# State-space outputs from four partial products, combined in PSUM by TensorE

## What is computed

```
_, _, x_re, x_im = lax.associative_scan(_ssm_combine, (a_re, a_im, bu_re, bu_im), axis=0)
y = (jnp.einsum('bsgp,ghp->bsgh', x_re, c_re.astype(f32))
     - jnp.einsum('bsgp,ghp->bsgh', x_im, c_im.astype(f32)))
y = y.reshape(bsz, s, S5_WIDTH) + d_skip.astype(f32) * uf
```

## Time and profile before

| | |
|---|---|
| time, median of 3 runs | 2228.7 us (2225.8 to 2232.6) |
| profiled execution, its own time | 2228.75 us |
| its span, first to last instruction | 2226.9 us |
| mean granted TensorE clock | 0.986 of full speed |
| busy: TensorE, VectorE, ScalarE, GpSimd | 97%, 68%, 45%, 32% |
| the four heads with state-space work | about 133 to 375 us of the span |

### The profile page before, as it was taken

One profiled execution on the slowest core, in us unless ns is written; L12 is line 12 of the kernel. 1 busy time (PEld: TensorE's weight loads), 2 busy tenths in 40 slices (PEclk: granted clock), 3 DMA queues, 4 the chain that ended last, 5 costly groups with the idle time before them and its releaser, 6 DMA issues.

```text
span 2226.9 us, 47155 instructions
## 1 busy us (share of the span) xinstructions
PE 2165.3 (97%) x18426; PEld 2134.6 (96%) x18426; DVE 1508.2 (68%) x1798; ACT 1005.2 (45%) x1244; POOL 708.4 (32%) x668
## 2 busy tenths in 40 slices
PE   8898889999999999999999999999999999999997
PEld 8888789999999999999999989999999999999997
DVE  6688896677666555666666666677666555666665
ACT  5333334545444444444444455444544444444442
POOL 4687771023434101434311000124343002343311
PEclk9999999999999999999999999999999999999998
DMA  6334334455555556545456433455554556454453
GB/s 261 141 138 145 125 137 172 160 198 176 207 192 191 169 195 215 201 177 206 162 195 219 161 120 136 161 201 190 185 198 177 182 198 215 184 207 180 173 192 116
DMA packets 64602, 398.68 MB, mean 179 GB/s; under 512 B 7168, under 2 KB 9728, under 8 KB 29056
## 3 DMA queue, kind: packets, MB, share of 16 engines
q1 hardware_dynamic: 60192, 391.15, 49.2%
q10 hardware_dynamic: 4320, 6.27, 0.9%
HBM read 395.29 MB, written 2.10 MB: 178 GB/s over the span
## 4 chain that ended last, share of the span: by engine, by line
PE 92%; DVE 4%; DVEq 2%; ACT 1%; issue 0%; DMA 0%; SPq 0%; ACTq 0%
PE PS L1492 27%; PE PS L1493 27%; PE PS L1496 27%; DVE lo L722 1%; DVEq L932 1%; PE PS L1590 1%; PE PS L1639 1%; PE PS L1487 1%; PE PS L1488 1%; PE PS L1489 1%; PE PS L1641 1%; PE PS L1640 1%; DVE S L948 1%; PE PS L1604 1%; ACT hi L363 0%
## 5 line engine op out<-in xcount | busy, mean ns | idle before, releaser
L722 DVE TENSOR_TENSOR lo<-raw,hi 128x1024 fp32r<-128x1024 f32 (+2 forms) x826 | 966.9, 1189 | 516.4 <-ACT hi L363 511.1
L363 ACT ACTIVATE hi<-raw 128x1024 fp32r<-128x1024 f32 (+2 forms) x826 | 787.2, 970 | 798.5 <-PE PS L1496 722.8
L1492 PE MATMUL PS<-XS,hi 128*128 128x256 f32 x3584 | 843.8, 278 | 8.6 <-ACT hi L363 8.6
L1493 PE MATMUL PS<-XS,hi 128*128 128x256 f32 x3584 | 838.4, 277 | 0.0
L1492 PEld LDWEIGHTS PS<-XS,hi 128*128 128x128 f32 x3584 | 674.3, 188 | 12.0 <-issue 11.6
L1493 PEld LDWEIGHTS PS<-XS,hi 128*128 128x128 f32 x3584 | 674.4, 188 | 0.4
L1496 PE MATMUL PS<-XS,lo 128*128 128x256 f32 x3584 | 481.0, 277 | 0.0
L1496 PEld LDWEIGHTS PS<-XS,lo 128*128 128x128 f32 x3584 | 441.4, 188 | 0.0
L1493 PE MATMUL PS<-YF,hi 128*128 128x256 f32 x1408 | 331.8, 276 | 0.0
L1492 PE MATMUL PS<-YF,hi 128*128 128x256 f32 x1408 | 331.8, 276 | 0.0
L1449 POOL TENSOR_TENSOR ctmp<-apad,cws 128x512 f32<-128x512 f32 x88 | 131.9, 1519 | 525.7 <-DVE apad L773 525.7
(11 more groups left out here) (259 smaller groups left out, 2465.0 us busy)
## 6 DMA issues: line engine op xcount, KB each, us to landing
raw<-in_ffn_up SPq DMA_DIRECT2D x176, 1024.0 KB, 4.8
raw<-in_ffn_dn SPq DMA_DIRECT2D x128, 704.0 KB, 4.1
raw<-in_w_in SPq DMA_DIRECT2D x51, 1024.0 KB, 4.8
raw<-in_w_oe SPq DMA_DIRECT2D x16, 1024.0 KB, 4.8
raw<-in_w_oo SPq DMA_DIRECT2D x16, 1024.0 KB, 4.8
raw<-in_mla_dn SPq DMA_DIRECT2D x9, 1024.0 KB, 4.8
raw<-in_w_ukv SPq DMA_DIRECT2D x8, 1024.0 KB, 4.7
raw<-in_w_uq SPq DMA_DIRECT2D x8, 768.0 KB, 4.3
```

The source lines that it names most:

```text
L363: act.activation(hi[:, p % SLOTS, 0:n], raw[:, u % SLOTS, off:off + n], ACT.Copy).then_inc(hi_ready, 1)
L722: V.tensor_tensor(lo[:, p % SLOTS, 0:n], raw[:, u % SLOTS, off:off + n], f(hi[:, p % SLOTS, 0:n]), ALU.subtract).then_inc(lo_ready, 1)
L1492: mm(PS[:, bank, 0:T], wh, x[:, 0:T], start=first, stop=False)
L1493: mm(PS[:, bank, 0:T], wh, x[:, T:2 * T], start=False, stop=False)
```

## The change

`Cst` gets a third plane. GpSimd writes the negated real part into it and the negated imaginary part over plane 1, as before; the load now writes runs of 64 values into a wider row. VectorE no longer forms the difference and the sum (L955, L956) nor the drain ahead of them, and raises `z_ready` behind the second product. `c_x` takes the four products as they are: C_re times s_re cos, -C_re times s_im sin, -C_im times s_re sin, -C_im times s_im cos, four matmuls per block instead of two, and goes through the two blocks in turn. Since `sB` is now read by `c_x`, the copy of new inputs into `sB` (bu_copy for an even m) waits for `c_done` of the half before and not for `z_ready`.

```
-        Cst = sb("Cst", [P, 4, 2, 32], fp32, even)
+        Cst = sb("Cst", [P, 4, 3, 32], fp32, even)
...
-                    act.dma_start(Cst[:, :, :, :].rearrange("p a b c -> p (a b c)"),
-                                  A["s5c"][h0 - 1, :, :] if r is None else
-                                  A["s5c"][ds(r + (h0 - 1), 1), :, :].rearrange("a p n -> p (a n)")).then_inc(cst_in, 16)
+                    act.dma_start(Cst[:, :, 0:2, :],
+                                  (A["s5c"][h0 - 1, :, :] if r is None else
+                                   A["s5c"][ds(r + (h0 - 1), 1), :, :].rearrange("a p n -> p (a n)"))
+                                  .rearrange("p (a b c) -> p a b c", a=4, b=2)).then_inc(cst_in, 16)
 
                 def bu_copy(m):
                     act.wait_ge(bu_done, S_(m + 1, 4))
                     if m % 2 == 0 and h0 - 1 + m > 0:
-                        act.wait_ge(z_ready, S_(m // 2, 2))
+                        act.wait_ge(c_done, S_(m // 2, 2))
...
                     V.tensor_tensor(sT2, sT1, eb[:, 0:1].broadcast_to([P, 2, 2, T]), ALU.mult)
-                    V.tensor_tensor(sB, sT1, eb[:, 1:2].broadcast_to([P, 2, 2, T]), ALU.mult)
-                    dve.drain()
-                    V.tensor_tensor(sT1[:, 0], sT2[:, 0], sB[:, 1], ALU.subtract)
-                    V.tensor_tensor(sT1[:, 1], sT2[:, 1], sB[:, 0], ALU.add).then_inc(z_ready, 1)
+                    V.tensor_tensor(sB, sT1, eb[:, 1:2].broadcast_to([P, 2, 2, T]), ALU.mult).then_inc(z_ready, 1)
...
                 pool.wait_ge(cst_in, at(16 * h0 + 16, 16, r))
+                G.tensor_tensor(Cst[:, :, 2, :], Cst[:, :, 0, :], minus[:, 0:1].unsqueeze(2).broadcast_to([P, 4, 32]),
+                                ALU.mult)
                 G.tensor_tensor(Cst[:, :, 1, :], Cst[:, :, 1, :], minus[:, 0:1].unsqueeze(2).broadcast_to([P, 4, 32]),
                                 ALU.mult).then_inc(cneg_ready, 1)
...
-                    for m in range(2):
-                        q = 2 * k + m
-                        for ri in range(2):
-                            ins = mm(PS[32 * q:32 * q + 32, 6, 0:T], Cst[:, q, ri, :], sT1[:, ri, m, :],
-                                     start=ri == 0, stop=ri == 1)
+                    for i, (c, x) in enumerate(((0, sT2[:, 0]), (2, sB[:, 1]), (1, sB[:, 0]), (1, sT2[:, 1]))):
+                        for m in range(2):
+                            q = 2 * k + m
+                            ins = mm(PS[32 * q:32 * q + 32, 6, 0:T], Cst[:, q, c, :], x[:, m, :], start=i == 0, stop=i == 3)
```

## The result

The changed kernel takes 2207.0 us (median, 2202.3 to 2210.1) against 2230.7 us (2225.8 to 2236.3) for the kernel before in the same comparison: a ratio of 0.9889, interval 0.9876 to 0.9902, or some 24 us less. I had forecast 11 us less; the time lies at the lower edge of my range of 2207 to 2229. The sign was right and the size was half of what came, because one step of the sum carried a duration over unchanged that didn't stay, and the count of half-clock spells hung on that step.

A forecast was written before the change was run, and what follows sets the result against it. VectorE's run up to c_x(0), and half clock behind TensorE's waits, were taken as the bound. Head 1 -1.7 - 3.3, matmuls +4.4, three turns -7.2, one spell -3.3: -11.1 us, 2217.5 us; range 2207 to 2229.

The forecast's parts named there:

- What bounds the kernel: TensorE waits 18.4 us in four places, c_x(0) of heads 1 to 4, for VectorE's sum, and restarts at half clock.
- Sums removed: Ahead of c_x(0): without L955, L956 and the drain, z_ready comes 1.73 us earlier in head 3.
- Matmuls added: In c_x on TensorE: doubled matmuls take 1.86 us, 0.87 more, at five exposed places: +4.4 us.
- Rival (c): In c_x: the new order stops matmuls running two at a time, 2.5 us more each; 2237 us, chance 0.07.
- (d): In c_x: the new order runs more matmuls at a time, so c_x stays at 0.99 us; 2213 us, chance 0.08.
- Wait added: At b_u(1) in heads 2 to 4: moving bu_copy(0) behind c_x(1) makes TensorE stand 0.75 us, out of slack.
- VectorE's run: VectorE's work up to c_x(0) ends last in a turn; heads 2 to 4 gain 2.4 us each by it.
- the walk: VectorE's run followed in head 3's times: L1029 0.7 us instead of 2.78, scan(0) 0.8 us early, z_ready at 259.5.
- The step that failed: From scan(0) to the end of L953 on VectorE: 7.66 us, as before.
- outer bound: Gain per turn if scan to L953 shrank from 7.66 to head 1's 5.99 us: about 4.1 us.
- The half clock: Behind c_x(0): head 1 keeps full clock, 3.3 us; one of three later spells goes, another 3.3 us.
- Rival (b): Heads 1 to 4: all half-clock spells go; 2211 us, up to 2207 with 3 us or more a turn; chance 0.20.

The follow-up runs named there:

- e1_sums_away: Kernel before without the two sums and their drain, end rotation left out of the result; 0.9905 of the kernel before, 21 us less.
- e8_sums_kept: Changed kernel with the drain, difference and sum kept ahead of z_ready, their result unused; 0.9958 of the kernel before, 9 us less.
- e6_block_by_block: Changed kernel with the eight matmuls of c_x issued block by block instead of in turn; 0.9912 of the kernel before.
- e12_sums_and_wait: Kernel before with sums away and bu_copy's wait moved, c_x keeping four matmuls, end rotation left out; 0.9894 of the kernel before.
- e3_wait_only: Kernel before with only the wait of bu_copy moved from z_ready to c_done; 0.9947 of the kernel before, 12 us less.
- e7_phasors_later: Changed kernel with GpSimd waiting for z_ready of the first half before making the second half's phasors; 0.9928 of the kernel before.
- e9_gpsimd_later: Kernel before with five tiny GpSimd writes ahead of the products of rotate_in(0) in heads 2 to 4; 0.9935, 14 us less.
- e4_clock_kept: Kernel before with six or eight unused full-width matmuls filling the idle time ahead of c_x(0); 0.9947, 12 us less.
- e2_matmuls_only: Kernel before with every matmul of c_x issued twice, sums and waits as before; 0.9953 of the kernel before, 10 us less.

## Why the prediction was half of it

**What bounds the kernel**: right. The time sat in four waits for VectorE and in the clock behind them.

**Sums removed**, 1.73 us a turn: right. In the changed kernel z_ready comes with the end of the product and TensorE follows 0.13 us later. I hadn't seen that this part decides: alone it gives 21 us (e1_sums_away), and the other two without it give 9 (e8_sums_kept).

**Matmuls added**, 1.86 us per c_x: right, 1.85 to 1.92. That they run two at a time in the new order was right; e6_block_by_block shows that the order isn't indifferent. Rival (c) didn't come, nor did (d), whose 0.99 us no c_x of sixteen records reached. What they cost in time, my +4.4 us, no run shows: e12_sums_and_wait has half of them and the same time.

**Wait added**, 0.75 us at b_u(1): right, 0.70. That it goes into slack was right, and said too little: alone it makes the kernel 12 us faster (e3_wait_only), since it starts GpSimd later.

**VectorE's run**, up to the scan: the direction was right, and L1027 at 0.69 us as walked. The scan came 1.26 us earlier against c_x(1), I had 0.8. Three readings were off: L1029 was ready at 237.3 and not at 236.3 (it starts at 237.34 in the earlier trace rows), GpSimd's first product came 1.9 us later against c_x(1) and not 1.65, and the walk's own 0.8 and 1.73 make 2.53 us a turn where the sum took 2.4.

**The step that failed** is the next one: "Then 7.66 us to the end of L953, as before". It was 5.78 to 6.0 us in all three heads. I had that value, from head 1, and used it for the outer bound only, because "the walk uses only durations of this head". But a duration that contains waits for GpSimd isn't a duration of the instruction: with GpSimd idle the same stretch took 4.87 us (e7_phasors_later). Once the walk had moved GpSimd against VectorE, every VectorE time beside GpSimd's work was open again, that one too. The traces now let me say it as a rule of this kernel. Over the three loop turns of thirteen kernels (all but e7_phasors_later), eleven turns have the head's output at 2.1 us or more, and all of these have 7.55 to 7.67 us from scan to product; twenty-eight have it at 0.69 us, and all of these have 5.77 to 6.06 us. There are two orders of taking turns, nothing between them was seen, and which it is hangs on whether VectorE starts its head's output before GpSimd starts its first product. The Trainium skill (SBUF — State Buffer, SBUF: two separate sides) has the rule behind it, an exclusive lock that the first to start holds for the whole instruction, if GpSimd's operation reads SBUF and VectorE's has two inputs there; these traces agree: 2.90 us where GpSimd started 0.04 us ahead, 0.69 us where it started 0.70 us behind. What the two orders cost, 3.6 to 3.7 us a turn in e9_gpsimd_later, only a run tells.

**The half clock**: priced about right (2.5 to 3.4 us a turn in e4_clock_kept, 3.3 taken from head 1) and counted wrong, one later spell gone instead of three. That follows from the failed step: with 1.7 us less a turn, and the scan another 0.46 us earlier, the wait of 2.3 us, where I couldn't tell, became 0.5 to 1.0 us, where I could. The clock of head 1 was kept as said, behind a wait of 0.68 us where I had 1.2, since its stretch from scan to product shrank too, from 5.99 to 5.40 us. My ground for it, that a wait of 2.0 us is short enough, was weaker than I took it for: the same wait lost the clock in three other kernels (last section). So the one spell in three that I took as gone was a guess, and no more.

In numbers, beyond the forecast: 3 x 1.67 for the stretch, 3 x 0.46 for the scan's start, 3 x 0.13 for the slip in the sum, two more spells at 3.3: 13.4 us. Forecast and these make 24.5, about what was measured. Rival (b), all spells gone and 3 us or more a turn, was the case that came; I had given it 0.20 and its good end, 2207, as the edge of the range.

**What stays open**: the slow matmuls of the odd layer's output projection in one profiled execution, and by how much a profiled execution in general differs from the median, since e2_matmuls_only took 2212.9 to 2224.1 us where the kernel before took 2226.5 to 2230.9 in the same comparison. Also open is why four and four matmuls of a block overlap only in part. A turn that is close to the other order can fall either way, which would do that; it wasn't shown.

## What to carry to other kernels

When a trace shows a small operation of VectorE at three times its usual length beside GpSimd, take apart what it is itself and what it waits, and price the change with the bare times and a fresh order of turns; don't carry the long times over. Try such a kernel with one engine held back by a microsecond before anything is rewritten: here five tiny writes gave more than half of what the change gave. And where TensorE waits for 2 to 5 us in every turn, the clock's share of it (3.3 us here) may be as large as the wait itself: what shortened the wait to 1.7 us or less, or filled it, got that as well here.

## What the runs showed of the hardware

**Waits of 1.8 to 2.7 us went either way with the clock.** TensorE in e2_matmuls_only, c_x(0) of head 3 behind a wait of 2.29 us:

```profile
255.13 1.92 PE L1604 MATMUL PS<-S,Cst 128*32 128x256 f32 x16 [2.29 <-DVE S L956]
```

The stretch that begins with it:

```profile
255.00:263.00 8.00, 7.87 (x55) 1.00 0.36 131
```

In e8_sums_kept the same matmuls behind a wait of 2.32 us:

```profile
253.15 2.70 PE L1607 MATMUL PS<-S,Cst 128*32 128x256 f32 x16 [2.32 <-DVE S L957]
```

And their stretch (in this row the clock stands behind the busy times of all engines):

```profile
253.00:261.00 8.00, 7.85 (x35) 5.42 (x36) 7.82 (x9) 0.60 (x1) 5.11 (x4) 0.57 0.35 117
```

The one stays at 2.4 GHz and the other spends most of its 8 us at 1.2 GHz. A shorter wait isn't safe either. The one of 1.96 us in the odd layer (L1487 in the kernel before), which I had taken as one that keeps the clock, does so in the kernel before, in the changed one and in nine others, and loses it in three. In e12_sums_and_wait:

```profile
1198.39 0.39 PE L1484 MATMUL PS<-XS,hi 128*128 128x256 f32 x1 [1.96 <-DVE XS L765]
```

And the stretch that begins 1.1 us behind it:

```profile
1199.50:1206.00 6.50, 6.50 (x43) 6.47 (x43) 2.45 (x2) 2.51 (x3) 0.00 (x0) 0.74 0.58 183
```

The shortest wait that lost the clock was one of 1.80 us, in e7_phasors_later, and the longest that kept it one of 2.67 us, in e2_matmuls_only. Over the traces of all fourteen kernels, waits of up to 1.75 us between matmuls kept it and those of 2.86 us and more lost it; between them the length of the wait alone doesn't decide.

**How far small matmuls overlap hangs on their order.** Two matmuls of one block followed by two of the other took 0.99 us; four and four took 2.74 to 2.81 us where the same eight in turn took 1.85 to 1.92. Had the four and four overlapped as the two and two did, it would have been the same 1.9.

**The scan is held up too.** L948 took 2.43 us for its four scans with no GpSimd beside it, 2.9 to 3.2 in the turns in the good order and 4.09 in those in the bad one (3.66 in one of them), like the products.
